# Layer norms whose sums are gathered while the residual is still being written

## The reference

```python
def layer_norm(x, g, b):
    xf = x.astype(jnp.float32)
    mu = jnp.mean(xf, axis=-1, keepdims=True)
    var = jnp.mean(jnp.square(xf - mu), axis=-1, keepdims=True)
    y = (xf - mu) * lax.rsqrt(var + NORM_EPS) * g.astype(jnp.float32) + b.astype(jnp.float32)
    return y.astype(x.dtype)
```

## Time and profile before

| | |
|---|---|
| median of 3 runs | 3211.32 us (3207.85 to 3218.03) |
| the profiled execution | 3210.9 us |
| its span in the profile | 3209.1 us |
| mean granted PE clock | 0.956 of full speed |
| busy PE / DVE / ACT / POOL | 2922.4 / 1684.3 / 1229.9 / 418.2 us |

### The profile page before, as it was taken

The page is one execution under the profiler, slowest core; times in us unless marked ns, Lnnn a source line. Parts: engine busy times, 40 slices in busy tenths (PEclk is TensorE's granted clock), DMA queues, the critical chain, the costliest instruction groups (busy, mean ns, idle before and its releaser), DMA issues. The chain is left out here.

```text
span 3209.1 us, 37054 instructions
## 1 busy us (share of the span) xinstructions
PE 2922.4 (91%) x14773; PEld 2312.8 (72%) x14773; DVE 1684.3 (52%) x2338; ACT 1229.9 (38%) x1821; POOL 418.2 (13%) x395
## 2 busy tenths in 40 slices
PE   7998899999979999999898799998999968876995
PEld 4886566888868888887686458886888736454874
DVE  3685665233346555543417554446656353655886
ACT  5334545122243211212526443225322244626884
POOL 4401400000100000002302100000000004202332
PEclk9999999999989999999899899999999988897997
DMA  6660101222114434432410104324656235433962
GB/s 209 162 178 24 24 1 50 59 61 69 53 34 137 129 108 116 121 87 51 87 52 16 24 15 105 97 73 139 193 165 179 72 53 67 159 117 136 374 239 79
DMA packets 397871, 330.12 MB, mean 103 GB/s; under 512 B 38038, under 2 KB 340484, under 8 KB 397572
## 3 DMA queue, kind: packets, MB, share of 16 engines
q1 hardware_dynamic: 384196, 304.56, 32.8%
q0 software_dynamic: 13248, 23.13, 3.0%
q10 hardware_dynamic: 256, 0.07, 0.0%
HBM read 331.96 MB, written 30.33 MB: 113 GB/s over the span
## 5 line engine op out<-in xcount | busy, mean ns | idle before, releaser
L1118 PE MATMUL ps<-ahi,w_hi 128*128 128x512 f32 (+1 forms) x2264 | 765.6, 352 | 8.1 <-DVE w_lo L1145 8.1
L1119 PE MATMUL ps<-ahi,w_lo 128*128 128x512 f32 (+1 forms) x2264 | 765.6, 352 | 0.0
L1145 DVE TENSOR_TENSOR w_lo<-w_raw,w_hi 128x1024 fp32r<-128x1024 f32 (+2 forms) x244 | 353.5, 1450 | 372.0 <-ACT w_hi L1135 369.7
L1118 PEld LDWEIGHTS ps<-ahi,w_hi 128*128 128x128 f32 x2264 | 427.3, 189 | 73.8 <-DVE w_lo L1145 11.0
L1121 PE MATMUL ps<-alo,w_hi 128*128 128x512 f32 (+1 forms) x2264 | 473.0, 351 | 0.0
L1119 PEld LDWEIGHTS ps<-ahi,w_lo 128*128 128x128 f32 x2264 | 427.6, 189 | 59.9
L1135 ACT CAST w_hi<-w_raw 128x1024 fp32r<-128x1024 f32 (+2 forms) x244 | 285.5, 1171 | 477.1 <-PE ps L1121 375.0
L1121 PEld LDWEIGHTS ps<-alo,w_hi 128*128 128x128 f32 x2264 | 376.2, 189 | 58.0
L885 DVE SCALAR_TENSOR_TENSOR vec_acc<-vec_w,csilu,vec_acc 128x512 f32<-128x512 f32 x364 | 261.9, 765 | 12.8 <-DMA vec_w<-in_w_mod 8.1
L1221 POOL TENSOR_TENSOR xsum<-x 128x768 f32<-128x768 f32 (+1 forms) x4 | 7.2, 1805 | 1403.1 <-DVE x L1206 1403.1
L1206 DVE SCALAR_TENSOR_TENSOR x<-ps,mod,x 128x512 f32<-128x512 f32 x80 | 51.4, 668 | 245.0 <-PE ps L1121 230.1
(11 more groups left out here) (529 smaller groups left out, 5183.2 us busy)
## 6 DMA issues: line engine op xcount, KB each, us to landing
vec_w<-in_w_mod SPq DMA_DIRECT2D x128, 512.0 KB, 3.9
w_raw<-in_w_in SPq DMA_DIRECT2D x102, 512.0 KB, 3.9
e_raw<-in_w_gate SPq DMA_DIRECT2D x46, 512.0 KB
e_raw<-in_w_up SPq DMA_DIRECT2D x46, 512.0 KB
e_raw<-in_w_down SPq DMA_DIRECT2D x46, 512.0 KB
w_raw<-in_w_ffn_gate SPq DMA_DIRECT2D x44, 512.0 KB, 3.8
w_raw<-in_w_ffn_up SPq DMA_DIRECT2D x44, 512.0 KB, 3.8
w_raw<-in_w_ffn_down SPq DMA_DIRECT2D x32, 704.0 KB, 4.7
```

The lines of the kernel that those rows point to most:

```text
L1118: pe.matmul(o, whi[:, j, b0 + b, :], hi[:, b, t0:t0 + tn], start=(b == 0), stop=False)
L1119: pe.matmul(o, wlo[:, j, b0 + b, :], hi[:, b, t0:t0 + tn], start=False, stop=False)
L1145: dve.tensor_tensor(wlo[:, j, 0:d.blocks, :], raw_of(d, i, jj), whi[:, j, 0:d.blocks, :].bitcast(F32), ALU.subtract).then_inc(lo_ready[j]. ...
```

## The change

For the three norms the sums are gathered inside the residual stage (class `Moments`), and about a provisional mean m0: the mean of the 128 channels of tile 0, made by PE (one product with ones) ahead of the third piece. DVE takes m0 away from every tile (tiles 0 to 3 after their eviction, tiles 4 to 7 before it), ACT squares tiles 0 to 6, and POOL keeps two running sums, of the tiles and of the squares: 12 additions where there were 6. After the last piece, before the barrier, PE adds both running sums into PSUM. At the head of the next block PE adds tile 7 and its square, ACT forms the remaining mean and its square, and DVE computes the variance as the mean square less that square. All eight tiles still have the remaining mean taken away by DVE (`recentred`): two early, the other six between the scalings.

The core of the diff:

```diff
@@ class Norm @@
             def pe(self, pe):
                 if self.counted:
+                    return
+                if self.running:
+                    for total, part, wait, done in ((self.sums, self.src[self.n - 1], None, norm_mean), (self.squares, self.sq[0], norm_sq, norm_var)):
+                        if wait is not None:
+                            pe.wait_ge(*self.sem(wait, 1))
+                        for t0, tn in self.tg:
+                            m = pe.matmul(total[:, t0:t0 + tn], ones[:], part[:, t0:t0 + tn], start=False, stop=True, skip_group_check=True)
+                        m.then_inc(done.sem, 1)
                     return
...
             def act_stats(self, act):
+                if self.running:
+                    act.activation(self.sq[0], self.src[self.n - 1], ACT.Square).then_inc(norm_sq.sem, 1)
+                    act.wait_ge(*self.sem(norm_mean, 1))
+                    act.activation(self.sq[1], self.sums, ACT.Identity, scale=-1.0 / self.dim).then_inc(norm_g.sem, 1)
+                    act.wait_ge(*self.sem(norm_g, 1))
+                    act.activation(self.tmp[0], self.sq[1], ACT.Square).then_inc(norm_g.sem, 1)
+                    return
...
+            def act_root(self, act):
+                act.activation(warm[:], ones[:, 0:1], ACT.Sqrt)
+                act.wait_ge(*self.sem(norm_rstd, 1))
+                act.activation(self.rstd, self.rstd, ACT.Sqrt, bias=ln_eps[:]).then_inc(norm_sqrt.sem, 1)
...
-                if self.center and not self.counted:
+                if self.running:
+                    dve.wait_ge(*self.sem(norm_g, 1))
+                    self.recentred(dve, 0)
+                    dve.wait_ge(*self.sem(norm_var, 1))
+                    dve.wait_ge(*self.sem(norm_g, 2))
+                    dve.scalar_tensor_tensor(out=self.rstd, in0=self.squares, scalar=1.0 / self.dim, in1=self.tmp[0],
+                                             op0=ALU.mult, op1=ALU.subtract).then_inc(norm_rstd.sem, 1)
+                    self.recentred(dve, 1)
+                elif self.center and not self.counted:
...
+            def recentred(self, dve, k):
+                dve.tensor_tensor(self.src[k], self.src[k], self.sq[1], ALU.add).then_inc(norm_x2[1].sem, 1)
+
+            def dve_root(self, dve):
+                dve.wait_ge(*self.sem(norm_sqrt, 1))
+                dve.reciprocal(self.rstd, self.rstd).then_inc(norm_rstd.sem, 1)
...
                 for k in range(0 if self.counted else ahead):
                     scaled(k)
+                    if self.running and k + 2 < self.n:
+                        self.recentred(dve, k + 2)
@@ run_dense @@
-                    for d, i, jj in () if presplit else pieces[0:2]:
-                        split(enter(d), i, jj)
+                    if isinstance(norm, Norm) and norm.running:
+                        split(enter(pieces[0][0]), *pieces[0][1:])
+                        {"act": norm.act_root, "dve": norm.dve_root}[who](eng)
+                        split(enter(pieces[1][0]), *pieces[1][1:])
+                    else:
+                        for d, i, jj in () if presplit else pieces[0:2]:
+                            split(enter(d), i, jj)
@@ class Moments (new) @@
+            CENTRED = {3: (0, 1, 2), 4: (3, 4), 5: (5, 6), 6: (7,)}
+            SQUARED = {4: (0, 1), 5: (2, 3), 6: (4, 5), 7: (6,)}
...
+            def pe(self, pe, p):
+                if p == 2:
+                    pe.wait_ge(*self.written(0))
+                    self.total(pe, self.first, x[:, 0, 0:self.T], True, True).then_inc(self.rough.sem, 1)
+                if p == KT:
+                    pe.wait_ge(*self.at(self.centred, KT))
+                    pe.wait_ge(*self.at(self.added, 2 * KT - 5))
+                    self.total(pe, self.sums, self.sum, True, False)
+                    pe.wait_ge(*self.at(self.added, 2 * KT - 4))
+                    self.total(pe, self.squares, self.square_sum, True, False)
+
+            def dve(self, dve, p):
+                for k in self.CENTRED.get(p, ()):
+                    if k == 0:
+                        dve.wait_ge(*self.at(self.rough, 1))
+                    if k <= 3:
+                        dve.wait_ge(*self.written(k))
+                    dve.scalar_tensor_tensor(out=x[:, k, 0:self.T], in0=self.first, scalar=-1.0 / P, in1=x[:, k, 0:self.T],
+                                             op0=ALU.mult, op1=ALU.add).then_inc(self.centred.sem, 1)
...
+            def act(self, act, p):
+                for k in self.SQUARED.get(p, ()):
+                    act.wait_ge(*(self.at(self.centred, k + 1) if k <= 3 else self.written(k)))
+                    if k >= 2:
+                        act.wait_ge(*self.at(self.added, max(2, 2 * (k - 2))))
+                    act.activation(self.sq[k % 2], x[:, k, 0:self.T], ACT.Square).then_inc(self.squared.sem, 1)
+
+            def pool(self, pool):
+                for k in range(1, KT - 1):
+                    pool.wait_ge(*(self.at(self.centred, k + 1) if k <= 3 else self.written(k)))
+                    if k >= 2:
+                        pool.wait_ge(*self.at(self.added, 2 * k - 3))
+                    pool.tensor_tensor(self.sum, x[:, 0, 0:self.T] if k == 1 else self.sum, x[:, k, 0:self.T], ALU.add).then_inc(self.added.sem, 1)
+                    pool.wait_ge(*self.at(self.squared, k + 1))
+                    if k >= 2:
+                        pool.wait_ge(*self.at(self.added, 2 * k - 2))
+                    pool.tensor_tensor(self.square_sum, self.sq[0] if k == 1 else self.square_sum, self.sq[k % 2], ALU.add).then_inc(self.added.sem, 1)
```

More of the change, by code:

```diff
@@ L1223, in presummed, with __init__, of, at @@
             return program
+        class Moments:
+            CENTRED = {3: (0, 1, 2), 4: (3, 4), 5: (5, 6), 6: (7,)}
+            SQUARED = {4: (0, 1), 5: (2, 3), 6: (4, 5), 7: (6,)}
+            def __init__(self, T, sq, square_sum):
+                self.T, self.sq, self.square_sum, self.sum = T, sq, square_sum, xsum[:, 0:T]
+                self.first, self.sums, self.squares = (ps[:, b * BANK:b * BANK + T] for b in (6, 2, 6))
+                self.rough, self.centred, self.squared, self.added = p_done[0], p_done[1], rs_done[1], sum_chain
+                self.c0 = {t: t.base for t in (self.rough, self.centred, self.squared, self.added)}
+            def of(self, layers):
+                self.d, self.n0 = layers[-1], sum(d.chunks for d in layers[:-1])
+                self.end = self.n0 + KT + 1
+                return self
+            def at(self, t, n):
+                return t.sem, self.c0[t] + n
+            def written(self, k):
+                t = psum_free[k % 2]
+                return t.sem, self.d.start[t] + k // 2 + 1
+            def total(self, pe, dst, part, start, stop):
+                for t0, tn in groups(self.T):
+                    m = pe.matmul(dst[:, t0:t0 + tn], ones[:], part[:, t0:t0 + tn], start=start, stop=stop, skip_group_check=True)
+                return m
+            def run(self, who, eng, n):
+                if who != "sp":
+                    {"dve": self.dve, "act": self.act, "pe": self.pe}[who](eng, n - self.n0)
+            def pe(self, pe, p):
[16 more added lines that the diff above has]
+                                             op0=ALU.mult, op1=ALU.add).then_inc(self.centred.sem, 1)
+            def before_out(self, dve, k):
+                if k >= 4:
+                    dve.wait_ge(*self.at(self.centred, k + 1))
+            def act(self, act, p):
[14 more added lines that the diff above has]
+                    pool.tensor_tensor(self.square_sum, self.sq[0] if k == 1 else self.square_sum, self.sq[k % 2], ALU.add).then_inc(self.added.sem, 1)
+            def ended(self):
+                self.rough.base += 1
+                self.centred.base += KT
+                self.squared.base += KT - 1
+                self.added.base += 2 * (KT - 2)
@@ L2333, in layer @@
                     layers += [swiglu(temps, loads, 2, NH, (ahi, alo), h, T),
-                               residual(mod, g["w_ffn_down"][l], 5 * KT, KT, h, T, row0=half * NH * P, nk=NH, needs=(Since(h_hi_ready, NH), Since(h_ready, NH)))]
-                g1, b1, g2, b2 = V_LN1_G + l * KT, V_LN1_B + l * KT, V_LN2_G + l * KT, V_LN2_B + l * KT
-                with ExitStack() as c1:
-                    vectors = (Vectors(c1, g["w_mod_2"][0], (2,), 0, vec3[:, 0:48], later, 4, start=2, norm_first=True) if last else
-                               Vectors(c1, g["w_mod"][l + 1], (0, 1), 0, vec2[:, (l + 1) * 48:(l + 2) * 48], later, 4, start=2, norm_first=True))
-                    room = vectors.raw[:].rearrange("p a b c -> p (a b c)")
-                    norm = Norm(c1, xt(T), T, LN_EPS, lambda k, m=1: col(vec1, g1 + k, m), (ahi, alo, *modulate_by(mod, 3)),
-                                [room[:, n * T:(n + 1) * T] for n in range(2)], temps[0][:], [temps[1][:], room[:, 0:T], room[:, T:2 * T]],
```

(7 more changed lines are left out.)

55 lines of the change are left out of this document (40 added, 15 removed).

## The result

The change is slower: 3228.04 us (median of five runs; 3226.8 to 3230.55) against 3211.32 (five runs too, where the table above says three), ratio 1.0047 with a 95% interval of 1.0034 to 1.006. I had forecast 3200 us, range 3192 to 3209. The profiled execution has a span of 3223.8 us, 14.7 more than before.

A forecast was written before the change was run, and what follows sets the result against it. PE, busy 91% of the span, was taken as the bound, with time to gain in the norms, a chain between ACT and DVE. Norms 1, 2 and 3 at -5.8, -3.6 and -1.4 sum to -10.8 us: 3200 us, range 3192 to 3209.

The forecast's parts named there:

- Norm 1, -5.8 us: Norm 1: PE dense 7.2 us earlier, less 1.4 us for the provisional mean in the residual stage.
- 13.4 us to the scaling: Norm 1: time from the block's opening to the start of the scaling, at 925.2 instead of 935.6.
- 42.5 to dense work: Norm 1: time from the block's opening at 911.8 until PE is dense again at 954.2.
- Norm 3, -1.4 us: Norm 3, 512 tokens: high pass ends 2.3 us earlier, less 0.9 us for the provisional mean.
- Norm 2, -3.6 us: Norm 2: -7.2, +4.8 for POOL's additions, -0.9 for splits, -1.7 for the low pass, +1.4 for the mean.
- the first term, "-7.2": Norm 2: PE dense again 7.2 us earlier, the figure worked out for norm 1.
- A landing later than 3.9: Sign of being wrong: weights landing later than 3.9 us, the landing time taken after the block opens.
- The last rival: Gain made but swallowed: DMA for third and fourth weights, or bias tables, hold PE later; 3209 us, chance 0.05.
- POOL's additions, 4.8 us: Norm 2: POOL's first eight bias additions fall into DVE's run of fourteen and cost 0.6 us each.
- the rival at 0.20: PE comes back slowly: its clock grant may stay at 1.2 GHz until the third piece; 3208 us, chance 0.20.
- POOL's chain end last: Rival: before the barrier, PE's totals wait for POOL's twelve additions; time near 3239 us, chance 0.06.
- The sum: Whole kernel: -5.8 - 3.6 - 1.4 = -10.8 us on 3210.9 us, giving 3200 us.

The follow-up runs named there:

- The run with norms 1 and 3 alone: Changed kernel with ln_eps sharing warm's slot, and the norm at the head of layer 1 as before the change; 3208.6 us, 0.9985 of the kernel before.
- the run with the shared slot: Changed kernel with ln_eps in the slot of warm, so every later tensor is back at its address of before; 3209.6 us, 1.0000 of the kernel before.
- The kernel before with POOL late: Kernel before the change, with POOL's layer 1 bias transfers begun only when the norm's last low part is written; ratio 0.9986 to the kernel before.
- the run where nothing else was moved: Kernel before the change, with the bias rows' landing place inside proj moved by 8 elements (32 bytes) and no tensor moved; ratio 1.0032.

## Why the prediction was wrong

- **Norm 1, -5.8 us: right.** 13.4 us to the scaling was 13.35, 42.5 to dense work was 42.9, the barrier 1.4 later where I had 1.7, the provisional mean 1.3 where I had 1.4. By the traces: -8.3 + 1.4 + 1.3 = -5.6 us.
- **Norm 3, -1.4 us: right.** The block opened at 2182.40 and PE was dense at 2213.33, 30.9 us against 34.3 before; with the later opening (0.9) and the mean (0.9) it gains 1.6. The run with norms 1 and 3 alone measured -4.8 us in place of -7.2, with an interval that reaches to -7.7.
- **Norm 2, -3.6 us: wrong.** The step that failed is the first term, "-7.2", taken over from norm 1 with its landing of 3.9 us and with the second tile's split at 1.2 directly behind the reciprocal. In norm 2 both tiles share the DMA engines with POOL's eight transfers. Before, the tiles' casts came behind the squares, at 1518.6, by when both had landed; the change wants the second one behind the reciprocal, which ended at 1515.5 in the run with the shared slot, and has no squares to cover its landing. I had costed the landing by a row of norm 1 alone. What the runs showed in its place: the second tile 15.9 us after the opening with the buffers in place and 18.5 in the changed kernel, and the scaling 4.0 and 6.3 us late by it. The other terms of norm 2 held, since -3.6 and -3.7 us are left when this wait is taken off. A landing later than 3.9 was among the signs of being wrong, and it came here. The last rival had the bias tables' DMAs in it, at 0.05, but for the weights behind the norm.
- **POOL's additions, 4.8 us: right in size.** Eight steps at 1.40 in place of 0.87 are 4.2 us, 0.53 each where I took 0.6. The Trainium skill, page "SBUF — State Buffer", section "Who interferes with whom", says that GpSimd and a VectorE instruction with two SBUF inputs exclude each other. The trace agrees that they take turns, and its 0.53 is less than the whole 0.75 of an addition by which I had weighed the rule. The prediction's twelve two-input instructions are a slip: the lists show sixteen (eight recentrings, eight scalings) where eight stood. No price hung on it.
- **PE's clock: no loss in norm 1.** The norms' windows show PEclk at 0.78 and 0.79 where the earlier trace rows had 0.84 and 0.86, but norm 1 was dense at the time forecast; the rival at 0.20 didn't come. In norm 2 it was 0.67 where the earlier trace rows had 0.75; I didn't price that. Nor did POOL's chain end last: its last addition ends at 913.7, ahead of the totals at 916.9.
- **The sum** left out a term, the second step that failed and the larger one: what happens to the program outside the change. I had put it at nothing, since its instructions are the same. It moved by 32 bytes and lost 0.47%, some 15 us. With the buffers in place the change measures 1.0000, still not the forecast. In the trace with the shared slot the norms give -5.0, +0.5 and -1.6 us, 6.1 in all, and the kernel ends 2.6 us ahead; the rest is lost in stretches between and behind them, and whether that is more than scatter stays open.
- **Luck.** With POOL's transfers behind the weights as well, the change measures 0.9966, 10.9 us faster. That is close to the -10.8 forecast, but not by my terms: norm 2 then gives 8.7 us (52.0 to 42.0, less 1.3 for the mean), and with norms 1 and 3 in that trace the terms come to 15. Some 4 us of them are lost again behind norm 2: the lead is 13.2 us at 1663 and 9.1 at 1930 (before's times). In that trace the granted clock from 1649.80 to 1772.40 was 0.93 to 0.94 (short spells at 1.2 GHz in work at 2.4), and in the same work before it was 1.00 and at last 0.96. The kernel before with POOL late shows the same loss, so it does not hang on the moments; what brings it on is open.

## What to carry to other kernels

An added buffer, however small, shifts all that is allocated behind it: compare the addresses before and after, keep what DMA reads and writes in small pieces on the multiples it had (here a shift by 128 bytes cost no time), and put new scalars into a slot that exists or behind everything else. When the first stretch of a trace is already late, ahead of any changed instruction, look there first. Where a chain gets shorter, list for each of its inputs when it arrives, not only when it was wanted before: the next one to come late may be a transfer that had been waiting.

## What the runs showed that I had not expected

- POOL's transfers into an address 32 bytes off a multiple of 256 land in 8.4 to 9.4 us (median), 8.7 in the run where nothing else was moved. On a multiple of 256 they land in 6.5 to 7.3, and in 7.6 to 7.7 in the two runs where `w_raw` lay 32 off and they did not; for 64 bytes off it was 8.4, for 128 bytes off 7.7.
- Moving the weight halves by 128 bytes against the moving operand slowed the 128x512 products from 392 to 397 ns (1.3%) and the kernel by 0.8%; moving both together cost nothing (1.0002). Moving the halves down by 8192 bytes or more left the pace at 393 ns. I didn't try other distances, and why 128 matters stays open. In the feed-forward part the halves had lain 192 bytes above a multiple of 256 and `ahi` on one.
- In the run where POOL waited for the weights, its first addition began inside the scaling and lasted 5.57 us, while the DVE steps stayed at 0.87 (ns min/median/max below); in the changed kernel and in the one with the shared slot the engines took turns, at 1.40 a step. Which of the two happens is not settled by these runs.

```profile
L1910 POOL TENSOR_TENSOR na_bias<-na_mask,proj x8: 742/1100/5572, 1523.6 to 1534.7; 128x256 f32<-128x256 f32 x8
```
